# Side-by-side 512-column matmuls in the first block, moved loads, and head norms with tokens on the partitions

## The chip, the cores and the metric

The kernel runs on one core of a Trainium2 chip, in one launch. The metric is the device time in microseconds, as a median of runs. Everything is fp32. A core has TensorE (matmuls, with a queue of weight loads beside it), VectorE, ScalarE, GpSimd and SyncE, each with its own instruction stream; here SyncE issues the large weight loads and GpSimd some of the rest.

## The reference

Two blocks over one sequence of T = 256 tokens, width 2048, batch 1. Cut to what matters:

```python
def first_block(x, c, ...):
    mod = silu(c) @ ada_w + ada_b                  # 2048 -> 12288; sh1, sc1, g1, sh2, sc2, g2
    h = rmsnorm(x, norm1_g) * (1 + sc1) + sh1
    q, kc, vc, ks, vs, kw, vw, g_nsa, lx, ly, ga, gb = split(h @ w_in)
    o_a = nsa_attention(...)                       # compressed, selected and window branch
    o_b = gelu(ly) * rg_lru(causal_dwconv(lx), ...)
    y = (sigmoid(ga) * (o_a @ proj_a) + sigmoid(gb) * (o_b @ proj_b)) @ w_out
    x = x + g1 * y
    h = rmsnorm(x, norm2_g) * (1 + sc2) + sh2
    gate, val = split(h @ w_up)                    # 2048 -> 2 x 6144
    x = x + g2 * ((gelu(causal_dwconv(gate)) * val) @ w_down)
    return rmsnorm(x, final_g)

def second_block(x, ...):
    q, k, v, a_gate, u, z, g_a, g_s = split(rms_norm(x) @ w_in)
    q = rms_norm(q.reshape(b, l, 16, 64), q_norm_w)     # over the 64 of each head
    k = rms_norm(k.reshape(b, l, 4, 64), k_norm_w)
    y_a = (window_attention(q, k, v) * silu(a_gate)) @ w_attn_proj
    glu_a, glu_b = split(gelu(s5_ssm(u, ...)) @ w_glu + b_glu)
    y_s = (glu_a * sigmoid(glu_b) * silu(z)) @ w_ssm_proj
    return x + (sigmoid(g_a) * y_a + sigmoid(g_s) * y_s) @ w_out
```

## The kernel before

Activations lie transposed in SBUF: features on the 128 partitions, in 16 chunks of 256 tokens. A product of fp32 precision is made of three matmuls: with a = a_hi + a_lo (each rounded to what TensorE multiplies exactly), x·w is x_hi·w_hi + x_lo·w_hi + x_hi·w_lo (L1792).

**Units and groups.** Weights stream from HBM in units of 512 KB, 256 input rows by 512 output columns, in a ring of ten slots (`wraw`) that SyncE fills in order. For each unit ScalarE writes the rounded half `whi` (L1267, four units ahead of TensorE, six buffers), VectorE the rest `wlo` (L1272, in place of the slot), and TensorE runs 24 matmuls: 2 chunks k × 4 output chunks o × 3 terms. Units make groups (`groups()`): a group has 512 output columns (four chunks) and 8 units, those of `down` 12, those with 1024 input rows 4. The order is k, v (with the compression), NSA gates, q, lx, ly, then four times ga, gb, pa, pb, then wout 0 to 3; for each of two FFN halves gate and val 0 to 5 in turn and down 0 to 3; then the second block: q2 0, kv2, u2 0, ag2 0, q2 1, u2 1, ag2 1, z2, ga2 0 to 3, pa2, gs2, gluA, gluB, ps2, wout2. Groups write to `pair0` and `pair1` in PSUM in turn (two banks each); four more banks serve the side work. After a group its evacuation (`evac`) brings PSUM to SBUF with the group's function: sigmoid on ScalarE, or a convolution with three taps on VectorE, for example, and then the split into hi and lo.

**ada.** The vector `mod` isn't computed on TensorE: rows of ada_w of 1 MB pass through two slots of the same ring, and VectorE multiplies each with silu(c) and sums (L1248), right behind the `wlo` of the unit that the row is tied to (`g.ada[s]`: slot s of group g). 32 of the 96 go ahead of the units; the others in three sets: 16 on k1, v1, q, lx, ly; 32 on ga, gb, pa, pb; 16 on gate and val 1 to 4 of the first half.

**Side jobs.** RG-LRU, NSA attention, the compression (L490 makes `blocks`, L499 multiplies them), the tables for the recurrence (`make_turns`, on GpSimd), the head norms of the second block, its attention and the recurrence (`states`) are jobs. Each is a generator with one step per unit: in each unit's turn every engine first does its part of the unit and then one step of each job that runs. `hand` gives work from one engine to another and goes on in the next unit. So the order on each engine is fixed in the program, and a late engine holds up what stands behind on its queue.

**Head norm** (`head_norm`, for q2 0, k2 and q2 1): squares, a matmul with `halves` that sums over each head's 64 partitions and spreads the sum over them (L811), a scale, the root on ScalarE (L818), RECIPROCALs of 128x256 on VectorE (L822), and one operation that multiplies (L827).

**bz and turns.** Before the recurrence GpSimd loads `turns` and `bz` (L1082, L1085) in the first step of `states`, in ag2 0; the first matmuls of the recurrence (L1097) read `bz`.

## Time and profile before

| | us |
|---|---|
| median of 3 runs | 2693.28 (2691.06 to 2696.19) |
| profiled execution | 2692.64 |
| span of its trace | 2690.9 |
| TensorE busy | 2597.1, 97% |
| VectorE busy | 1877.7, 70% |
| ScalarE busy | 1107.6, 41% |
| GpSimd busy | 227.3, 8% |

DMA moves 568.13 MB at a mean 211 GB/s. Busy time of TensorE counts matmuls that overlap in the pipeline, so a stretch of it is read by its starts: how many matmuls begin in how many microseconds. The groups of rows below are from the page (the summary of one execution), from windows (busy time of each engine in a stretch, with the granted clock of TensorE as a share of full speed), from timelines (start, length, engine, line, operation; in square brackets the idle time of the engine before it and what ended it) and from the chain of waits that ended last.

### The profile page before, as it was taken

To read this page: it belongs to the slowest core of one execution; us is meant where nothing else is said; L and a number is where in the kernel's file an instruction comes from. 1 tells how busy PE (TensorE), PEld (TensorE's weight loads), DVE (VectorE), ACT (ScalarE), POOL (GpSimd) and SP (SyncE) were. 2 spreads that over 40 slices of the span, in tenths; PEclk is the share of its full clock that TensorE was granted. 3 is DMA by queue.
4 is the path that set the end of the run, shared out by engine and by line. 5 is a ranking of instruction groups with operands and counts; after the bars stand their busy time and mean duration, and the time that the engine had idled before them with its cause. 6 is when DMAs were issued, how large, how long until landed. Compare 5 with 4: busy or idle time off the path is not lost.

```text
span 2690.9 us, 48148 instructions
## 1 busy us (share of the span) xinstructions
PE 2597.1 (97%) x20256; PEld 2505.2 (93%) x20256; DVE 1877.7 (70%) x2519; ACT 1107.6 (41%) x1381; POOL 227.3 (8%) x190
## 2 busy tenths in 40 slices
PE   7999999989999999899999999999999999999999
PEld 5789999889999999899999999999999888899999
DVE  7865667676866674679976556654487898898563
ACT  1033456455333344444443344444444444534432
POOL 0000000000000001000466610001100000000000
PEclk9988999999999999999999999999999999999999
DMA  9974466456888886478866766665555554465664
GB/s 404 424 269 151 156 204 188 142 157 212 274 268 275 278 276 211 134 254 274 278 225 212 221 211 181 183 185 180 165 181 180 157 162 132 149 189 176 195 197 134
DMA packets 243462, 568.13 MB, mean 211 GB/s; under 512 B 17424, under 2 KB 21520, under 8 KB 228784
## 3 DMA queue, kind: packets, MB, share of 16 engines
q1 hardware_dynamic: 233776, 530.33, 60.9%
q0 software_dynamic: 9472, 34.74, 3.6%
q8 instruction: 160, 2.62, 0.4%
q14 instruction: 54, 0.44, 0.1%
...
## 4 chain that ended last, share of the span: by engine, by line
PE 75%; DVE 12%; DVEq 4%; DMA 3%; ACT 3%; issue 2%; SPq 0%; ACTq 0%; POOL 0%
PE pair L1792 65%; DVE wlo L1272 4%; DMA wraw<-ada_wT_dram 3%; ACT whi L1267 2%; DVE wraw L1248 1%; PE pair L1365 1%; PE bank L499 1%; PE pair L1798 1%; DVEq L338 1%; PE pair L1785 1%; PE states_in L684 1%; PE bank L1365 1%; PE states_in L1370 1%; PE states_in L1097 0%; PE pair L1803 0%
## 5 line engine op out<-in xcount | busy, mean ns | idle before, releaser
L1272 DVE TENSOR_TENSOR wlo<-wraw,whi 128x1024 fp32r<-128x1024 f32 x777 | 977.6, 1267 | 586.0 <-ACT whi L1267 559.5
L1267 ACT ACTIVATE whi<-wraw 128x1024 fp32r<-128x1024 f32 x777 | 813.4, 1057 | 1163.9 <-PE pair L1792 669.7
L1792 PE MATMUL pair<-h_hi,whi 128*128 128x256 f32 x3936 | 1136.3, 289 | 22.2 <-DVE h_lo L426 9.2
L1792 PE MATMUL pair<-h_lo,whi 128*128 128x256 f32 x3936 | 1121.5, 285 | 0.0
L1792 PE MATMUL pair<-h_hi,wlo 128*128 128x256 f32 x3936 | 1120.8, 285 | 0.0
L1792 PEld LDWEIGHTS pair<-h_hi,whi 128*128 128x128 f32 x3936 | 763.6, 194 | 41.5 <-issue 34.9
L1792 PEld LDWEIGHTS pair<-h_lo,whi 128*128 128x128 f32 x3936 | 763.9, 194 | 0.6
L1792 PEld LDWEIGHTS pair<-h_hi,wlo 128*128 128x128 f32 x3936 | 763.1, 194 | 0.0
L1248 DVE SCALAR_TENSOR_TENSOR wraw<-wraw,cb 128x2048 f32<-128x2048 f32 x96 | 221.4, 2309 | 58.1 <-DMA wraw<-ada_wT_dram 56.8
L1792 PE MATMUL pair<-hid_hi,whi 128*128 128x256 f32 x768 | 218.5, 284 | 0.0
L1792 PE MATMUL pair<-hid_hi,wlo 128*128 128x256 f32 x768 | 217.3, 283 | 0.0
L1792 PE MATMUL pair<-hid_lo,whi 128*128 128x256 f32 x768 | 217.3, 283 | 0.0
L1792 PEld LDWEIGHTS pair<-hid_lo,whi 128*128 128x128 f32 x768 | 147.4, 192 | 0.2
L1792 PEld LDWEIGHTS pair<-hid_hi,whi 128*128 128x128 f32 x768 | 147.4, 192 | 0.2
L1792 PEld LDWEIGHTS pair<-hid_hi,wlo 128*128 128x128 f32 x768 | 147.4, 192 | 0.0
L1792 PE MATMUL pair<-m_hi,whi 128*128 128x256 f32 x512 | 145.5, 284 | 0.0
L1792 PE MATMUL pair<-m_lo,whi 128*128 128x256 f32 x512 | 144.9, 283 | 0.0
L1792 PE MATMUL pair<-m_hi,wlo 128*128 128x256 f32 x512 | 144.9, 283 | 0.0
L1792 PEld LDWEIGHTS pair<-m_lo,whi 128*128 128x128 f32 x512 | 98.3, 192 | 0.1
L1792 PEld LDWEIGHTS pair<-m_hi,whi 128*128 128x128 f32 x512 | 98.3, 192 | 0.1
L1792 PEld LDWEIGHTS pair<-m_hi,wlo 128*128 128x128 f32 x512 | 98.3, 192 | 0.0
L1365 PEld LDWEIGHTS pair<-h_f,wfour 128*128 128x128 f32 x256 | 49.1, 195 | 29.0 <-issue 22.6
...
## 6 DMA issues: line engine op xcount, KB each, us to landing
wraw<-w_in_dram SPq DMA_DIRECT2D x312, 512.0 KB, 3.7
...
wraw<-ffn_up_dram SPq DMA_DIRECT2D x192, 512.0 KB, 3.7
...
```

Source lines behind the costliest of these rows:

```text
L338: return ve.drain() if self.me == "dve" else None
L499: ins = te.matmul(bank[1][:, 0, 0:60], wcmp[which][:, l, :], blocks[:, l, :], start=(l == 0), stop=(l == 31))
L684: te.matmul(bank[3][:, 0, :], vv(br, 0), pt[:, br, 0:T], start=False, stop=False, skip_group_check=True)
L1248: ve.scalar_tensor_tensor(out=row, in0=row, scalar=1.0, in1=cb[:, :], op0=ALU.mult, op1=ALU.mult, accum_out=mod[:, col:col + 1]).then_inc( ...
L1267: sc.activation(whi[:, r, 0:w], wraw[:, PLACE[z], 0:w], ACT.Copy).then_inc(hi_ready, 1)
L1272: ve.tensor_tensor(wlo[:, PLACE[z], 0:w], wraw[:, PLACE[z], 0:w], whi[:, r, 0:w].bitcast(F32), ALU.subtract).then_inc(lo_ready, 1)
L1365: ins = te.matmul(out, w[:, g * CB + o * P:g * CB + (o + 1) * P], x, start=(c == 0 and o % 2 == 0), stop=(c == DC - 1), skip_group_check=True)
L1370: ins = te.matmul(flat(bank[2 + b][:, :, :]), x[:, b * P:(b + 1) * P], w[:, 3 * CB:4 * CB], start=(c == 0), stop=(c == DC - 1))
L1785: ins = te.matmul(pair[:, 2 * b, 0:48], x[:, b * P:(b + 1) * P], w[:, k * 48:(k + 1) * 48], start=(k == 0 and t == 0), stop=(k == 15 and t ...
L1792: ins = te.matmul(pair[:, o, :], w[:, at_w + o * P:at_w + (o + 1) * P], x, start=(k == 0 and o % 2 == 0 and t == 0), stop=(k == last and t ...
L1798: ins = te.matmul(flat(pair[:, 2 * b:2 * b + 2, :]), x[:, b * P:(b + 1) * P], w[:, at_w:at_w + CB], start=(k == 0 and t == 0), stop=(k == ...
```

## The change

There are five parts.

1. **Wide groups.** 41 groups (pb 0 to down 3 of the first FFN half without wout, and gate and val of the second half) keep the hi and lo halves of the activations side by side, `[P, n, 2, T]`, so that one matmul of 512 columns multiplies `whi` with both, into one PSUM bank per output chunk; a matmul of 256 columns adds w_lo·x_hi to the first half of the bank. The evacuation first copies the second halves to SBUF (`tl`, ScalarE), adds the two on VectorE into `tl`, and goes on from there, two steps later than before. PSUM is cut anew for it: two areas of four banks, of which the last two serve the side work in other times.
2. **ada rows.** The first set is tied to q, ly (one each) and lx (two each), none to k1, v1. The third is tied to wout 0 (two), wout 1, wout 2 and to slot 2 of each gate and val of the first half, so also to gate 0.
3. **Head norm.** The squares are the stationary side of matmuls with two columns of `halves`, so that the sums come with tokens on the partitions, 128x16; scale, root and reciprocal work on these. VectorE spreads the result over 64 columns a head, and a matmul with the identity turns it back, from which two operations multiply q (for k2 half of each). There are two hand-offs more.
4. **First turns.** The loads of `bz` and `turns` are a job of their own, from the third unit of q2 0, ahead of the spill of outT on GpSimd's queue, `bz` first.
5. **The LRU output's last quarter** is split from `lr` itself.

TensorE in pb 0, the product of one unit; `ob` is the LRU output, `pair` and `banks` are PSUM. Before:

```order
3596 L1792 MATMUL pair<-ob_lo,whi 128x256
3597 L1792 MATMUL pair<-ob_hi,wlo 128x256
3598 L1792 MATMUL pair<-ob_hi,whi 128x256
3599 L1792 MATMUL pair<-ob_lo,whi 128x256
3600 L1792 MATMUL pair<-ob_hi,wlo 128x256
3601 L1792 MATMUL pair<-ob_hi,whi 128x256
3602 L1792 MATMUL pair<-ob_lo,whi 128x256
3603 L1792 MATMUL pair<-ob_hi,wlo 128x256
```

and of the change:

```order
2623 L1840 MATMUL banks<-ob,whi 128x512
2624 L1842 MATMUL banks<-ob,wlo 128x256
2625 L1840 MATMUL banks<-ob,whi 128x512
2626 L1842 MATMUL banks<-ob,wlo 128x256
2627 L1840 MATMUL banks<-ob,whi 128x512 [waits lo_ready]
2628 L1842 MATMUL banks<-ob,wlo 128x256
2629 L1840 MATMUL banks<-ob,whi 128x512
2630 L1842 MATMUL banks<-ob,wlo 128x256
```

Three matmuls for a product are now two.

VectorE in k1 and v1, around the first operations of the compression (`blocks`). Before:

```order
133 L1248 SCALAR_TENSOR_TENSOR wraw,mod<-wraw,cb 128x2048 [waits w_loaded8]
134 L1272 TENSOR_TENSOR wlo<-wraw,whi 128x1024 [waits hi_ready,consts_made]
135 L1416 COPY k_71<-bank 128x512 [waits pe_units]
136 L1416 COPY k_71<-bank 128x512
137 L1416 COPY v_72<-states_in 128x512 [waits pe_units]
138 L1416 COPY v_72<-states_in 128x512
139 L1272 TENSOR_TENSOR wlo<-wraw,whi 128x1024 [waits hi_ready] x2
140 L1272 TENSOR_TENSOR wlo<-wraw,whi 128x1024 [waits hi_ready,pair_freed0]
141 L1248 SCALAR_TENSOR_TENSOR wraw,mod<-wraw,cb 128x2048 [waits w_loaded4]
142 L490 TENSOR_SCALAR blocks<-kc_73,vec 128x60 x8
```

and of the change:

```order
133 L1301 TENSOR_TENSOR wlo<-wraw,whi 128x1024 [waits hi_ready,consts_made]
134 L1457 COPY k_64<-banks 128x512 [waits pe_units]
135 L1457 COPY k_64<-banks 128x512
136 L1457 COPY v_65<-banks 128x512 [waits pe_units]
137 L1457 COPY v_65<-banks 128x512
138 L1301 TENSOR_TENSOR wlo<-wraw,whi 128x1024 [waits hi_ready] x2
139 L1301 TENSOR_TENSOR wlo<-wraw,whi 128x1024 [waits hi_ready,pair_freed0]
140 L502 TENSOR_SCALAR blocks<-kc_66,vec 128x60 x8
```

The two ada operations, each of which waits for a load into the ring, are gone from ahead of `blocks`.

VectorE in the middle of the head norm of q2 0, between the recurrence's own operations (L11xx, L12xx). Before:

```order
1309 L1272 TENSOR_TENSOR wlo<-wraw,whi 128x1024 [waits hi_ready]
1310 L822 RECIPROCAL t_70<-t_70 128x256 [waits act_to_dve]
1311 L822 RECIPROCAL t_70<-t_70 128x256
1312 L1178 TENSOR_TENSOR wr<-turns_102,sy 128x512
1313 L1179 TENSOR_TENSOR wi<-turns_102,sx 128x512
1314 L1181 TENSOR_TENSOR si<-wr,wi 128x512
1315 L1272 TENSOR_TENSOR wlo<-wraw,whi 128x1024 [waits hi_ready]
1316 L822 RECIPROCAL t_70<-t_70 128x256 x2
1317 L1272 TENSOR_TENSOR wlo<-wraw,whi 128x1024 [waits hi_ready]
1318 L827 SCALAR_TENSOR_TENSOR q_104<-q_104,vec,t_70 128x1024
```

and of the change:

```order
1361 L1301 TENSOR_TENSOR wlo<-wraw,whi 128x1024 [waits hi_ready]
1362 L837 RECIPROCAL ltmp<-ltmp 128x16 [waits act_to_dve]
1363 L839 COPY t_62<-ltmp 128x1024
1364 L1207 TENSOR_TENSOR wr<-turns_95,sy 128x512
1365 L1208 TENSOR_TENSOR wi<-turns_95,sx 128x512
1366 L1210 TENSOR_TENSOR si<-wr,wi 128x512
1367 L1301 TENSOR_TENSOR wlo<-wraw,whi 128x1024 [waits hi_ready] x2
1368 L850 SCALAR_TENSOR_TENSOR q_97<-q_97,vec,banks 128x512 [waits pe_to_dve]
1369 L850 SCALAR_TENSOR_TENSOR q_97<-q_97,vec,banks 128x512
```

Four large RECIPROCALs are one small one and a copy, and the multiplication comes one unit later.

The diff, cut to its core:

```diff
-    at = [(out[of(kind, 1)], s) for kind in ("k", "v") for s in (1, 3)]
-    at += [(out[of("q", i)], 1) for i in range(4)] + [(out[of(kind, i)], 1) for i in range(4) for kind in ("lx", "ly")]
+    at = [(out[of("q", i)], 1) for i in range(4)] + [(out[of("ly", i)], 1) for i in range(4)]
+    at += [(out[of("lx", i)], s) for i in range(4) for s in (1, 3)]
...
-    at = [(out[of(kind, i)], s) for i in range(1, 5) for kind in ("gate", "val") for s in (1, 3)]
+    at = [(out[of("wout", i)], s) for i, s in ((0, 1), (0, 3), (1, 1), (2, 1))]
+    at += [(out[of(kind, i)], 2) for i in range(6) for kind in ("gate", "val")]
...
+    for g in range(of("pb", 0), of("down", 3, 0) + 1):
+        out[g].wide = out[g].kind != "wout"
+    for g in range(of("gate", 0, 1), of("val", 5, 1) + 1):
+        out[g].wide = True
...
-        return put(name + "_hi", at, [P, n, T], F32R), put(name + "_lo", at + n * 1024, [P, n, T], F32R)
+
+        both = put(name, at, [P, n, 2, T], F32R)
+        return both[:, :, 0, :], both[:, :, 1, :], both
...
-    pairs = [ctx.enter_context(nc.psum_tensor(f"pair{n}", [P, 4, T], F32)) for n in range(2)]
-    bank = [ctx.enter_context(nc.psum_tensor(f"bank{n}", [P, 2, T], F32)) for n in range(2)]
-    states_in = ctx.enter_context(nc.psum_tensor("states_in", [P, 2, 2, T], F32))
-    bank += [states_in[:, 0], states_in[:, 1]]
+
+
+    wides = [ctx.enter_context(nc.psum_tensor(f"banks{n}", [P, 4, 2, T], F32)) for n in range(2)]
+    pairs = [w[:, 0:2, :, :].rearrange("p b c t -> p (b c) t") for w in wides]
+    bank = [wides[n // 2][:, 2 + n % 2, :, :] for n in range(4)]
+    states_in = wides[1][:, 2:4, :, :]
...
+        w = 4 * n
...
-                ins = te.matmul(bank[c // 2][:, c % 2, :], halves[:, :], t1[:, c, :], start=True, stop=True)
+                for b in range(2):
+                    at = 4 * c + 2 * b
+                    ins = te.matmul(bank[0][:, 0, at:at + 2], t1[:, c, b * P:(b + 1) * P], halves[:, 0:P:64], start=True, stop=True)
         yield from j.hand("pe_to_dve", "pe", "dve", ins)
         if me == "dve":
-            for c in range(0, n, 2):
-                ins = ve.tensor_scalar(t2[:, c:c + 2, :], bank[c // 2][:, :, :], 1.0 / 64, EPS, ALU.mult, ALU.add)
+            ins = ve.tensor_scalar(hroot[:, 0:w], bank[0][:, 0, 0:w], 1.0 / 64, EPS, ALU.mult, ALU.add)
         yield from j.hand("to_act", "dve", "act", ins)
         if me == "act":
-            ins = sc.activation(t2[:, 0:n, :], t2[:, 0:n, :], ACT.Sqrt)
+            ins = sc.activation(hroot[:, 0:w], hroot[:, 0:w], ACT.Sqrt)
         yield from j.hand("act_to_dve", "act", "dve", ins)
-        for c in range(n):
-            if me == "dve":
-                ve.reciprocal(t2[:, c, :], t2[:, c, :])
-            if c % 2:
-                yield
-        if me == "dve":
-            ve.drain()
-            ve.scalar_tensor_tensor(out=src, in0=src, scalar=V(name), in1=t2[:, 0:n, :], op0=ALU.mult, op1=ALU.mult)
+        if me == "dve":
+            ve.reciprocal(hroot[:, 0:w], hroot[:, 0:w])
+            ve.drain()
+            ins = ve.tensor_copy(t1[:, 0:n, :].rearrange("p c (h r) -> p (c h) r", r=64),
+                                 hroot[:, 0:w].unsqueeze(2).broadcast_to([P, w, 64]))
+        yield from j.hand("to_pe", "dve", "pe", ins)
+        if me == "pe":
+            for c in range(n):
+                for b in range(2):
+                    ins = te.matmul(bank[c // 2][:, c % 2, b * P:(b + 1) * P], t1[:, c, b * P:(b + 1) * P], ident[:, :],
+                                    start=True, stop=True)
+        yield from j.hand("pe_to_dve", "pe", "dve", ins)
+        if me == "dve":
+            for c in range(0, n, 2):
+                ve.scalar_tensor_tensor(out=src[:, c:c + 2, :], in0=src[:, c:c + 2, :], scalar=V(name),
+                                        in1=bank[c // 2][:, :, :], op0=ALU.mult, op1=ALU.mult)
...
+    def first_turns(j):
+
         j.sync("to_pool", "dve", "pool", j.drained())
-        if me == "pool":
+        if j.me == "pool":
+            po.wait_ge(pe_units, U1[of("down", 3, 1)])
             po.wait_ge(turns_out, 256)
             for n in range(2):
+                load_bz(n)
                 load_turns(n)
-                load_bz(n)
+        yield
...
+        if gr.wide:
+
+            e, w = tl, wides[g % 2]
+            yield from j.hand("to_act", "dve", "act", j.drained())
+            if computed("act"):
+                ins = sc.activation(tl[:, :, :], w[:, :, 1, :], ACT.Copy)
+            yield from j.hand("act_to_dve", "act", "dve", ins)
+            if me == "dve":
+                done(ve.tensor_tensor(tl[:, :, :], w[:, :, 0, :], tl[:, :, :], ALU.add))
+                ve.drain()
+            done = lambda ins: ins
...
+    job(first_turns, start_of("q2", 0) + 2)
...
+                if gr.wide:
+                    for o in range(4):
+                        out, cols = wides[g % 2][:, o, :, :], slice(at_w + o * P, at_w + (o + 1) * P)
+                        te.matmul(out, wh[:, cols], X[gr.x][2][:, k, :, :], start=(k == 0), stop=(k == last),
+                                  skip_group_check=True)
+                        ins = te.matmul(out[:, 0, :], wl[:, cols], hi[:, k, :], start=False, stop=(k == last),
+                                        skip_group_check=True)
+                elif "T" in gr.mode:
```

## Rows read from the trace of the kernel before

**Rows 1.** The page, part 4: shares of the span on the chain that ended last
```profile
PE 75%; DVE 12%; DVEq 4%; DMA 3%; ACT 3%; issue 2%; SPq 0%; ACTq 0%; POOL 0%
```

**Rows 2.** Engines by stage: us, PE, PEld, DVE, ACT, POOL busy, PEclk, DMA share, GB/s
```profile
688.00:1000.00 312.00, 312.00 (x2600) 312.00 (x2601) 214.11 (x184) 122.74 (x119) 0.00 (x0) 1.00 0.82 273
1199.00:1291.00 92.00, 92.00 (x769) 92.00 (x768) 84.90 (x175) 40.10 (x43) 0.00 (x0) 1.00 0.80 274
1291.00:1318.00 27.00, 24.40 (x201) 24.05 (x201) 26.00 (x28) 8.48 (x8) 11.17 (x7) 1.00 0.75 253
1318.00:1387.00 69.00, 69.00 (x577) 69.00 (x576) 57.81 (x52) 31.51 (x35) 45.97 (x28) 1.00 0.79 261
1525.00:1802.00 277.00, 277.00 (x2311) 277.00 (x2310) 166.09 (x189) 118.80 (x127) 24.82 (x19) 1.00 0.65 193
```

**Rows 3.** Timeline of TensorE inside a 256-column unit: start us, length us
```profile
1600.24 0.28 PE L1792 MATMUL pair<-h_hi,whi 128*128 128x256 f32 x1
1600.36 0.28 PE L1792 MATMUL pair<-h_lo,whi 128*128 128x256 f32 x1
```

**Rows 4.** Timeline of TensorE, 512-column matmuls of the v group
```profile
195.14 0.39 PE L1798 MATMUL pair<-wlo,h_hi 128*128 128x512 f32 x1
...
205.11 0.39 PE L1798 MATMUL pair<-whi,h_lo 128*128 128x512 f32 x1
```

**Rows 5.** The page, part 5, and the timeline of VectorE: two prices
```profile
L1248 DVE SCALAR_TENSOR_TENSOR wraw<-wraw,cb 128x2048 f32<-128x2048 f32 x96 | 221.4, 2309 | 58.1 <-DMA wraw<-ada_wT_dram 56.8
1250.61 1.21 DVE L1500 TENSOR_TENSOR t<-t,pair 128x1024 f32<-128x1024 f32 x1
```

**Rows 6.** Timelines of VectorE and TensorE in gate 4 of the first half
```profile
1303.15 2.13 DVE L1272 TENSOR_TENSOR wlo<-wraw,whi 128x1024 fp32r<-128x1024 f32 x1 [0.18 <-issue]
1311.12 0.36 PE L1792 MATMUL pair<-h_hi,whi 128*128 128x256 f32 x1 [2.15 <-DVE wlo L1272]
```

**Rows 7.** Timelines of VectorE and TensorE in gate 0 of the first half
```profile
1113.31 1.23 DVE L1272 TENSOR_TENSOR wlo<-wraw,whi 128x1024 fp32r<-128x1024 f32 x1 [0.95 <-ACT whi L1267]
1117.28 1.23 DVE L1272 TENSOR_TENSOR wlo<-wraw,whi 128x1024 fp32r<-128x1024 f32 x1 [0.95 <-ACT whi L1267]
1116.38 0.39 PE L1792 MATMUL pair<-h_hi,whi 128*128 128x256 f32 x1 [0.62 <-DVE h_lo L426]
```

**Rows 8.** The chain in order of time, 130 to 245 us: start us, us, what
```profile
146.70 12.90 DMA wraw<-ada_wT_dram
171.24 13.91 PE bank L499 x64
185.15 6.70 PE pair L1798 x24
234.29 7.09 PE bank L499 x64
```

**Rows 9.** Timeline of TensorE, and the window of the half clock around it
```profile
171.24 1.11 PE L499 MATMUL bank<-blocks,wcmp 128*128 128x60 f32 x4 [3.57 <-DVEq L338]
170.40:187.50 17.10, 16.26 (x70) 15.78 (x71) 8.81 (x12) 2.76 (x4) 0.00 (x0) 0.50 0.03 11
```

**Rows 10.** The chain in order of time, lx 0: an ada operation on it
```profile
415.65 2.20 DVE wraw L1248
```

**Rows 11.** The start of the recurrence: timeline of TensorE, then the chain
```profile
2038.25 0.80 PE L1097 MATMUL states_in<-u,bz 32*128 32x256 f32 x2 [3.13 <-DMA bz<-B_dram]
2038.25 2.08 PE states_in L1097 x8
2040.33 25.01 PE pair L1792 x192
```

**Rows 12.** Head norms: groups by line, timeline of TensorE, then the chain
```profile
L822 DVE RECIPROCAL t<-t 128x256 f32<-128x256 f32 x10 | 16.8, 1720 | 0.1
2222.96 0.58 PE L842 MATMUL bank<-kg,q 64*128 64x128 f32 x1 [5.26 <-DVEq L338]
1989.36 1.73 PE bank L811 x8
2224.61 7.75 PE pair L1792 x48
```

48 lines of the change are left out of this document (28 added, 20 removed).

## The prediction

> **What bounds the kernel now.** I read three views of the profile in this order: the shares of the chain that ended last, the busy time by stage, and the timelines around each gap of TensorE. The chain lies on TensorE for 75% of the span and on VectorE for 12% [rows 1]. By stage, TensorE is busy without a break for 312 us and again for 277 us, in which one matmul per 0.120 us runs (2600 in 312 us) [rows 2]. There the number and width of the matmuls alone set the time, and what VectorE and ScalarE do costs nothing. So two things can bring time: cheaper matmuls, and gaps. The gaps that the change touches are few: the compression of k and v, gate 0 of the first FFN half, gate 4 of it, the start of the recurrence, and the head norm before the last attention. The prologue's 140 us and nearly all of the other gaps stay.
>
> **Wide matmuls.** The 41 wide groups have 344 units of 8 products each, 2752 in all: pb 0 to down 3 of half 0 without wout (13 + 12 + 4 groups; 104 + 96 + 48 units) and gate and val of half 1 (12 groups, 96 units). A product is now three 256-column matmuls, and becomes one of 512 columns and one of 256. The columns streamed are the same, 768; one matmul is saved. Inside a unit the 256-column matmuls start 0.12 us apart [rows 3]; 312 us for 2600 makes it 0.120 [rows 2]. The nearest row for the other form is in group v, whose matmuls take 512 columns: 44 of them lie between 195.14 and 205.11 us, so 9.97 / 44 = 0.2266 each [rows 4]. A product goes from 3 × 0.120 = 0.360 to 0.2266 + 0.120 = 0.3466, which saves 0.0133 us; × 2752 = 36.7 us. I take 13 ns, 35.8 us, and subtract the 64 products of gate 0 (0.8), where another chain sets the pace (below): **−35.0**. The two ends are −29 (if mixing the two widths costs 2 to 3 ns per product) and −37. In sentences of its own: the Trainium skill, "TensorE: Matmul & The Clock Gate", section "Back-to-back issue gap", says that back-to-back matmuls are columns / 2.4 GHz plus about 2.5 ns apart; the rows show 13 ns for both widths. By the page's figure one matmul less is worth 2.5 ns and the whole part 6.9 us, by the rows 35.8; the measurement decides.
>
> **What the wide groups add beside it.** Each of the 41 evacuations gets a ScalarE copy of the second half of the columns to SBUF and a VectorE addition before the work of before. The nearest row for a VectorE operation of 128x1024 with one operand in PSUM is 1.21 us [rows 5]; with its drain I take 1.35 us. Where TensorE is busy throughout it is hidden: in 688 to 1000 us VectorE is busy 214 of 312, in 1525 to 1802 166 of 277 [rows 2], and 1.35 + about 1.1 of waiting per group of 23 us changes neither. The banks of a group are then free two units after the next one's start, six before they are wanted. pb 3's longer end moves the issue of the x reload some 6 us, which its reader in wout 0 has as slack: 0, with 2 us if not. The split of the last quarter of the LRU output from `lr` costs a drain. The addition isn't hidden by much in the first FFN half: 84.9 of 92 us busy at 1199 to 1291 [rows 2], or 21.3 us in a group of 23.04 (192 × 0.120), and the group now takes 22.2 (64 × 0.3466). Against the addition stand the ada operations that leave. Two of these (1 MB, 2.31 us each [rows 5]) leave each gate and val group from 1 to 4 and one comes back: −2.31 + 1.35 = −1 us of VectorE per group, to which the two new hand-offs may add 1 us in which VectorE waits for ScalarE. I take 0. The one gap of that stretch, 2.15 us where matmuls wait for `wlo` [rows 6], is made by GpSimd's make_turns, next to which a VectorE subtraction takes 2.13 us where it took 1.23 [rows 6, 7]; VectorE is busy 26.0 of 27 us there, and 57.8 of 69 behind it [rows 2]. I leave it as it is: 0, with +12 (1 us in each of 12 groups not absorbed) and −3 (the gap gone) as ends.
>
> **Loads moved out of k1, v1.** In the stage of the chain from 130 to 245 us a 1 MB ada load of 12.90 us stands on the chain, and then the 64 matmuls of compress for k take 13.91 us where those for v take 7.09, and the 24 behind them 6.70 where 24 × 0.2266 = 5.44 would do [rows 8]. Before the first of them TensorE idles 3.57 us for VectorE's `blocks`, and in 170.4 to 187.5 us the granted clock is 0.50, so the level of 1.2 GHz [rows 9]. The order of VectorE shows what `blocks` waits for: an ada operation directly before them, and another some rows above, both behind late loads. With it gone, the idle time (3.57), the half clock (13.91 − 7.09 = 6.82) and its rest (1.26) should go: 11.65 in all. What stands in the way is that the weights of the next units come from the same queue, which may be the next to be late; I take **−10**, and the ends are 0 (the clock falls anyway) and −11.65. The four loads go to lx, where the chain leaves TensorE at times; one ada operation of 2.20 us stands on it in that stage [rows 10]. Four more cost between 0 and 4 × 2.31 = 9.2 us. Since one of the dozen there now is on the chain, I take that one of the four will be: **+2**.
>
> **Loads moved in the FFN.** Gate 0 of half 0 gets one. Its units are paced by a chain on VectorE of 3.97 us (1113.31 to 1117.28) with TensorE idle 0.62 us before a unit's first matmul [rows 7], so nothing hides the 2.31 us: **+2.3**. The four in wout 0 to 2 and those in the others lie beside TensorE that is busy: 0.
>
> **bz and turns earlier.** At the recurrence's start the matmuls wait 3.13 us for `bz`, and then the 8 take 2.08 us and the next 192 take 25.01 [rows 11], where 192 × 0.120 = 23.04: 3.13 + 1.04 (half of 2.08, at half clock) + 1.97 = 6.1. The loads now start at the third unit of q2 0, three groups (some 70 us) earlier. GpSimd then waits until `down` 3 of half 1 is done; what is queued behind on it is the spill of outT and later turns, whose first reader is the recurrence: 0. What is late next: the states' own VectorE chain. **−6.1**, ends 0 and −6.1.
>
> **Head norms.** A RECIPROCAL of 128x256 takes 1.72 us, and there are ten: four in each q2 norm and two in k2's [rows 12]. The one of q2 1 ends in an idle time of TensorE of 5.26 us before attention, after which 48 matmuls take 7.75 us [rows 12] instead of 5.76, so 7.3 us with the clock's part. New on VectorE: 1 of 128x16, a copy of 128x1024 and two STT of 128x512 in place of four RECIPROCALs and one STT: about 6.9 + 1.2 before, some 2.5 now, less two more hand-offs (each up to a unit's 2.9 us). The gap of 5.26 ends with VectorE's queue; 5.6 less work there is enough to close it: **−7.3**, ends 0 and −7.3. On TensorE the norm gets dearer: 8 records of the 256-column fp32 matmul take 1.73 us [rows 12]; now 8 matmuls of 2 columns and 8 of 128 columns, two records each. The nearest small-column row is 64 records of 60 columns in 7.09 us [rows 8], 111 ns each: 32 × 0.111 = 3.55, +1.8 for each of two q2 norms, +0.9 for k2: **+4.5** (0 if the small ones overlap other waits).
>
> **Sum.** −35.0 − 10 + 2 + 2.3 − 6.1 − 7.3 + 4.5 = −49.6. The profiled run took 2692.64 us (span 2690.9), 0.6 below the median of 2693.28; 2692.6 − 49.6 = 2643.0, against the median 2643.6: I predict **2644 us**.
>
> **The rivals.**
> (1) A gap closes and another takes its place. TensorE's gaps at compress, bz and the last head norm are each set by the last of several waits; what hands over instead is VectorE with its own chain. For it: in each of the three, VectorE's queue holds the waiting work [rows 8, 11, 12]. Against it: 5.6 us leave VectorE at the norm. Two of the three lost are −8 to −17 of the sum: 2652 to 2661.
> (2) VectorE sets the pace in the first FFN half. It is busy 92% there [rows 2], and faster units (22.2 instead of 23 us per group) bring it nearer. If the new hand-offs are not absorbed: +8 to +12, 2652 to 2656; with the gap at make_turns wider, up to 2664.
> (3) More is won: the gap at gate 4 goes (−3), the four loads in lx cost nothing and the norm's small matmuls fall into waits (−4): 2626 to 2636.
> (4) The matmuls' fixed cost isn't 13 ns in the mixed form, and a product keeps within 2.5 ns of its 0.360: 6.9 of 35.8 is left, 2672. For it is the page's figure alone; against it, both widths in the rows [rows 3, 4].
> (5) It doesn't do what it says: the wide matmul brings nothing and additions cost nothing; 2644 + 35 = 2679.
> (6) **Slower than before.** VectorE becomes the bound in all 25 wide groups up to down 3 of half 0 (13 + 12). This decides when a group needs over 22.2 + 4 us of VectorE: the 49.6 us saved / 12 FFN groups = 4.1 us per group. From 84.9 / 92 a group has now 21.2 us of 23, plus drains; −1 + 1 in hand-offs makes 21.2 to 23. It would need the operations slowed beside GpSimd (2.13 for 1.23 [rows 6, 7]) in the whole half, where GpSimd is busy for 57 us of the 188 [rows 2]. 2695 or more.
>
> **How the numbers follow.** The forecast (2634 to 2655) 0.55; (1) 0.15; (2) 0.13; (3) 0.08; (4) 0.04; (5) 0.02; (6) 0.02; within 0.2% (which is about what a measurement of this kernel can tell from no change, 5 us) 0.01. Range: from 2629 (most of (3)) to 2664 (all of (1) and (2)); (4) to (6) are left out. All of the cases but (6) and the last lie more than 5.4 us below 2693.28: faster 0.96, same 0.02, slower 0.02.
>
> **What would show it right or wrong.** Wide part: 8 products of a unit in 2.77 us instead of 2.88, so 104 units of pb 0 to pb 3 some 11 us shorter; wrong if the 512-column one stands 0.24 from its neighbour. Compress: 64 matmuls for k in 7.1 us at granted clock 1.00, no idle time of 3 us before; wrong if the clock is still 0.50 from 170 us. bz: the 8 state matmuls wait under 1 us. Norm: no RECIPROCAL of 128x256 left and under 1 us of idle time before the last attention. FFN: idle time of TensorE between gate 1 and val 5 of half 0 under 5 us in all; over 10 is rival (2). The forecast is wrong in its main step if TensorE's busy stretches keep 0.120 us per 256 columns.

## The result, and the profile after

| | before | after |
|---|---|---|
| median, us | 2693.65 (2691.06 to 2696.19, 5 runs) | 2667.18 (2658.68 to 2670.79, 5 runs) |
| ratio | | 0.9898, 95% interval 0.988 to 0.9915 |
| span of the profiled execution, us | 2690.9 | 2665.4 |

The change makes the kernel 1.0% faster, by 26 us, where 1.8% (49 us) was forecast, and the time lies 3 us above the range. The runs of after also lie twelve microseconds apart, those of before five.

The page of after, parts 1 and 4 (busy time, share of the span, instructions; then the chain that ended last):

```profile
PE 2570.9 (96%) x17564; PEld 2352.7 (88%) x17564; DVE 1917.3 (72%) x2556; ACT 1142.0 (43%) x1422; POOL 225.4 (8%) x190
...
PE 72%; DVE 13%; DVEq 5%; ACT 4%; issue 3%; DMA 3%; SPq 0%; ACTq 0%; POOLq 0%; POOL 0%
```

TensorE executes 2692 instructions fewer, but VectorE has more of the chain than in [rows 1]: not all of what the matmuls gave back arrives at the end.

To see where, I took from both traces the start of the first matmul of each group and subtracted. This is the length of a stretch after less its length before, in us, beside the terms of the prediction:

```
stretch                         measured   predicted
start to pa 0                       -9.6       -8.0    (compress -10, ada in lx +2)
pb 0 to pb 3          (wide)        -5.6      -11
wout 0 to 3                         +2.2        0
gate 0, half 0        (wide)        +2.1       +2.3
val 0 to val 5        (wide)        -1.2       -9
down 0 to 3, half 0   (wide)        -2.6       -5
gate, val of half 1   (wide)        -5.1      -10
down 0 to 3, half 1                  0          0
q2 0 to u2 0                        +2.8       +2.7    (small matmuls of two head norms)
ag2 0                               -5.9       -6.1    (bz)
q2 1 to ga2 0                       -4.5       -5.5    (the last head norm)
ga2 1 to the end                    +1.9        0
sum                                -25.5      -49.6
```

Six of the twelve stretches came within 1.6 us of their terms, −15.1 us together for −14.6. What failed are four of the five wide stretches, −14.5 for −35.0, with 2.2 and 1.9 us at two smaller places. The last 1.9 us needs care: 1.5 of it are in pa 2 0, a group that takes 12.8 us in some executions and 14.2 to 14.3 in others, with either head norm (below).

Windows of after in wide stretches (columns as in [rows 2]: us, then busy us and number of instructions of PE, PEld, DVE, ACT, POOL, then the granted clock, the DMA share, GB/s):

```profile
700.00:980.00 280.00, 280.00 (x1587) 242.77 (x1586) 205.70 (x177) 119.92 (x117) 0.00 (x0) 1.00 0.80 278
1120.00:1250.00 130.00, 130.00 (x751) 113.68 (x750) 105.05 (x178) 71.44 (x78) 0.00 (x0) 1.00 0.72 231
1511.00:1780.00 269.00, 269.00 (x1524) 233.39 (x1523) 179.15 (x198) 129.06 (x138) 10.55 (x10) 1.00 0.65 194
```

Two matmuls are a product. The first row gives 280 / (1587 / 2) = 0.353 us for one, the third 0.353 too, and the second 0.346. TensorE is busy all the time and the clock is granted in full in all three. From the starts of the matmuls the two values are 0.3533 and 0.3467: the second is what was forecast. So the same instructions run at one of **two paces**, 6.7 ns apart. Over the trace, by units of eight products, 262 units have the slower pace, 63 the faster, and 17 hold a stall. The pace never changes inside a stretch without a stall: slow from pb 0 (690 us), fast from val 0 (1119.5), slow, fast and slow again among the stalls of 1252 to 1355, and then slow to the end of half 1.

The stalls of the first half, on the waits of TensorE in 1252 to 1378 us (total, times, longest):

```profile
PE banks L1840 <- DVE wlo L1301: 7.3, 6, 2.2
```

and one place of VectorE's timeline in gate 4:

```profile
1286.31 1.23 DVE L1301 TENSOR_TENSOR wlo<-wraw,whi 128x1024 fp32r<-128x1024 f32 x1
1287.76 2.13 DVE L1301 TENSOR_TENSOR wlo<-wraw,whi 128x1024 fp32r<-128x1024 f32 x1 [0.23 <-issue]
1289.82 3.15 DVE L1277 SCALAR_TENSOR_TENSOR wraw<-wraw,cb 128x2048 f32<-128x2048 f32 x1
```

At 1287.75 GpSimd begins make_turns, and the same subtraction takes 2.13 instead of 1.23 us, the ada operation 3.15 instead of 2.3. Before, the waits for `wlo` in this part were 2.6 us in two, the 2.15 of [rows 6] among them; now they are 7.3 us in six. By groups, gate 4 has lost 4.0 us against its term, gate 5 2.7 and val 3 1.0.

In wout 1, VectorE's timeline and then TensorE's:

```profile
1011.93 2.29 DVE L1277 SCALAR_TENSOR_TENSOR wraw<-wraw,cb 128x2048 f32<-128x2048 f32 x1 [5.78 <-DMA wraw<-ada_wT_dram]
```

```profile
1023.51 0.70 PE L385 MATMUL banks<-t,ones 128*128 128x256 f32 x2 [1.97 <-POOLq L379]
```

VectorE stands for 5.78 us behind an ada load that the change put there, and so res, the squares on GpSimd and the sum on TensorE are late.

At the compression, the chain and two windows, and between them one window of before; then the recurrence's start and the head norm (TensorE's timelines), and the norm's operations by line:

```profile
166.50 7.09 PE banks L511 x64
```

```profile
211.40:225.10 13.70, 13.70 (x66) 13.70 (x66) 11.49 (x54) 2.59 (x3) 0.00 (x0) 0.50 0.16 51
```

```profile
195.75:216.23 20.48, 20.48 (x98) 20.48 (x98) 11.73 (x54) 2.73 (x4) 0.00 (x0) 0.50 0.10 31
170.40:187.50 17.10, 17.10 (x92) 14.67 (x92) 6.08 (x6) 5.20 (x6) 0.00 (x0) 1.00 0.29 87
```

```profile
2018.14 1.14 PE L1121 MATMUL banks<-u,bz 32*128 32x256 f32 x8
...
2170.28 1.97 PE L828 MATMUL banks<-halves,t 128*128 128x2 f32 x16 [0.79 <-DVE t L822]
```

```profile
L850 DVE SCALAR_TENSOR_TENSOR q<-q,vec,banks 128x512 f32<-128x512 f32 x4 | 2.8, 743 | 2.9 <-PE banks L845 2.9
L839 DVE COPY t<-ltmp 128x1024 f32<-128x1024 f32 (+1 forms) x3 | 1.8, 605 | 0.2
```

The 64 matmuls for k take 7.09 us (13.91 in [rows 8]) at full clock: the half clock of [rows 9] is gone. A second one, which neither [rows 9] nor the prediction shows, was there before too, in 211.40 to 225.10 us, over the second part of the NSA gates and the start of q 0. Now it begins 15.7 us earlier, 3 us after the gates do, and lasts 20.48 us for 13.70; the gates take 17.7 us for 15.0. In the other traces with the loads moved it lasts 13.7 to 20.5 us and the gates 14.9 to 17.8, so this loss varies between executions. The norm's two multiplications take 0.74 us each and the copy that spreads 0.6 on average over its two widths, where a RECIPROCAL took 1.72. The state matmuls have no wait for bz (3.13 us in [rows 11]) and take 1.14 us for 2.08.

### The profile page after: what moved, and what is told of

Read it like the earlier page. It is cut to its first block, busy times and chain, and to the rows that moved or that the text cites. A ratio compares the mean times of both kernels' runs of the same rounds, so it can differ in the third digit from the quotient of the medians.

```text
span 2665.4 us, 42959 instructions
## 1 busy us (share of the span) xinstructions
PE 2570.9 (96%) x17564; PEld 2352.7 (88%) x17564; DVE 1917.3 (72%) x2556; ACT 1142.0 (43%) x1422; POOL 225.4 (8%) x190
## 4 chain that ended last, share of the span: by engine, by line
PE 72%; DVE 13%; DVEq 5%; ACT 4%; issue 3%; DMA 3%; SPq 0%; ACTq 0%; POOLq 0%; POOL 0%
PE banks L1847 33%; PE banks L1840 20%; PE banks L1842 10%; DVE wlo L1301 5%; DMA wraw<-ada_wT_dram 2%; ACT whi L1296 2%; PE banks L1394 2%; DVEq L350 1%; PE banks L1853 1%; PE banks L1833 1%; DVE wraw L1277 1%; PE banks L511 1%; PE banks L720 1%; PE banks L696 1%; PE banks L1399 1%
## 5 line engine op out<-in xcount | busy, mean ns | idle before, releaser
L1847 PE MATMUL banks<-h,whi 128*128 128x256 f32 x4032 | 751.3, 288 | 7.8 <-DVE h L434 7.8
L1840 PE MATMUL banks<-h,whi 128*128 128x512 f32 x1920 | 679.4, 399 | 18.5 <-DVE h L438 11.2
L1847 PEld LDWEIGHTS banks<-h,whi 128*128 128x128 f32 x4032 | 635.3, 194 | 25.1 <-issue 22.7
L1847 PE MATMUL banks<-h,wlo 128*128 128x256 f32 x2016 | 573.3, 284 | 0.0
L1842 PE MATMUL banks<-h,wlo 128*128 128x256 f32 x1920 | 538.8, 281 | 0.0
L1840 PEld LDWEIGHTS banks<-h,whi 128*128 128x128 f32 x1920 | 362.0, 189 | 109.8 <-issue 16.4
L1847 PEld LDWEIGHTS banks<-h,wlo 128*128 128x128 f32 x2016 | 390.0, 193 | 0.0
L1842 PEld LDWEIGHTS banks<-h,wlo 128*128 128x128 f32 x1920 | 363.8, 189 | 0.0
L1277 DVE SCALAR_TENSOR_TENSOR wraw<-wraw,cb 128x2048 f32<-128x2048 f32 x96 | 221.9, 2314 | 35.6 <-DMA wraw<-ada_wT_dram 34.3
L1847 PE MATMUL banks<-hid,whi 128*128 128x256 f32 x768 | 139.6, 284 | 0.0
L1840 PE MATMUL banks<-hid,whi 128*128 128x512 f32 x384 | 135.7, 399 | 0.0
L1847 PEld LDWEIGHTS banks<-hid,whi 128*128 128x128 f32 x768 | 120.2, 192 | 0.4
L1847 PE MATMUL banks<-hid,wlo 128*128 128x256 f32 x384 | 108.7, 283 | 0.0
L1842 PE MATMUL banks<-hid,wlo 128*128 128x256 f32 x384 | 107.8, 281 | 0.0
L1847 PE MATMUL banks<-m,whi 128*128 128x256 f32 x512 | 92.9, 284 | 0.0
L1840 PEld LDWEIGHTS banks<-hid,whi 128*128 128x128 f32 x384 | 72.2, 188 | 18.1
```

What stands on the lines that cost most here:

```text
L1277: ve.scalar_tensor_tensor(out=row, in0=row, scalar=1.0, in1=cb[:, :], op0=ALU.mult, op1=ALU.mult, accum_out=mod[:, col:col + 1]).then_inc( ...
L1840: te.matmul(out, wh[:, cols], X[gr.x][2][:, k, :, :], start=(k == 0), stop=(k == last), skip_group_check=True)
L1842: ins = te.matmul(out[:, 0, :], wl[:, cols], hi[:, k, :], start=False, stop=(k == last), skip_group_check=True)
L1847: ins = te.matmul(pair[:, o, :], w[:, at_w + o * P:at_w + (o + 1) * P], x, start=(k == 0 and o % 2 == 0 and t == 0), stop=(k == last and t ...
```

## The experiments

Each time is set against runs of before that were taken beside it. Their median is 2692.8 for the first four experiments, 2696.2 for the next four, 2693.5 for the three behind them and 2696.5 for the last three. Where two experiments are compared, it is by these distances.

**The changed kernel once more (x1_again).** No edit.

> The changed kernel once more, for a second trace. In its first trace a product (one 512- and one 256-column matmul) takes 0.3533 us in 262 wide units and 0.3467 us in 63, and the pace changes only behind a stall of TensorE. Theory P (TensorE keeps one of two paces, taken at random when it starts again behind a stall): 2659 to 2671 us, and other stretches than before at 0.3467. Rival Q (traffic of VectorE or DMA beside it sets the pace of a stretch): the same stretches have the same pace as in the first trace (val 0 to val 3 of half 0 at 0.3467, pb 0 to pb 3 and half 1 at 0.3533), 2667 us.

Measured: 2672.86 us (2668.2 to 2674.63), 19.9 below before. The stalls of half 0 are larger: TensorE's gate 5 lasts 28.0 us (24.9 in the first trace) and down 0 36.6 (33.9). The paces lie as in the first trace, which is what Q expects and P doesn't; the time lies above both. One repetition doesn't settle it (x4_turns_late does). The waits for `wlo` are 11.3 us in seven here, for 7.3 in six, so the stall varies by some 4 us between executions.

**No wide groups (x2_narrow).**

```diff
-        out[g].wide = out[g].kind != "wout"
+        out[g].wide = False
...
-        out[g].wide = True
+        out[g].wide = False
```

> No group is wide: three 256-column matmuls a product everywhere, without the copy and addition; the rest of the change stays. From the trace of after the wide products gain 2752 x 13.3 ns = 36.6 us less 262 x 8 x 6.7 ns = 14.0 us, so 22.6. Theory A (the copies and additions made the larger stall in gate 4 and 5 of half 0, 8 us more than before): 2667 + 22.6 - 8 = 2682. Rival B (the moved loads made it): it stays, 2667 + 22.6 = 2690.

Measured: 2675.56 us, 17.2 below before. TensorE has no wait for `wlo` at all in 1252 to 1378 us, fewer than before, and 700 to 980 and 1120 to 1380 run at 0.120 us:

```profile
700.00:980.00 280.00, 280.00 (x2336) 280.00 (x2335) 188.50 (x162) 107.09 (x103) 0.00 (x0) 1.00 0.81 274
1120.00:1380.00 260.00, 260.00 (x2169) 259.96 (x2168) 211.88 (x313) 120.20 (x132) 63.68 (x39) 1.00 0.75 240
```

Theory A holds for the mechanism: GpSimd works here too, and it stalls nothing. The tables and make_turns hurt only together with the wide groups. The run takes away two things at once, though: the additions, and the faster pace of TensorE, which gives VectorE 22.2 to 22.6 us for a group where it has 23.0 here. Their shares aren't separated. In time it is 6 us below A's 2682, since I hadn't counted the 3.0 us that the gap of [rows 6] gives back when the ada loads of gate 1 to 4 are halved, and the 1.5 us of wout 1 (24.2 us here, 25.7 in after); the rest is within what executions of one kernel differ by. The wide part as shipped is thus worth only 3 to 9 us, and the rest of the change 17.

**Order of the widths (x3_hifirst).**

```diff
-                    for o in range(4):
-                        te.matmul(out, wh[:, cols], X[gr.x][2][:, k, :, :], ...)
-                        ins = te.matmul(out[:, 0, :], wl[:, cols], hi[:, k, :], ...)
+                    for o in range(4):
+                        te.matmul(wides[g % 2][:, o, :, :], wh[:, cols(o)], X[gr.x][2][:, k, :, :], ...)
+                    for o in range(4):
+                        ins = te.matmul(wides[g % 2][:, o, 0, :], wl[:, cols(o)], hi[:, k, :], ...)
```

> In a wide unit, for each k, the four 512-column matmuls come first and then the four 256-column ones, so that the widths alternate twice in eight and not eight times. Theory P (the slower pace belongs to the alternation of widths): all wide units at 4 x (0.2267 + 0.120) = 1.387 us for four products, 14 us less, 2653. Rival Q (traffic beside it): the paces of the stretches stay as in after, 2667 within 3.

Measured: 2666.23 us, 26.5 below before. The time is Q's, but the stretches show that neither holds: in all of them a product takes 0.350 or 0.351 us. The 512-column matmuls in a row start 0.229 to 0.236 us apart, not 0.2266 as in [rows 4]. The order does change the pace, to one between the two, and the stalls of half 0 stay (waits for `wlo` of 10.5 us; gate 5 27.8 us, down 0 36.2).

**make_turns later (x4_turns_late).**

```diff
-    job(make_turns, end_of("val", 3), end_of("val", 3) + 2)
-    job(output_factors, start_of("gate", 2, 1), end_of("val", 3, 1))
+    job(make_turns, start_of("down"), start_of("down") + 2)
+    job(output_factors, start_of("gate", 4, 1), end_of("val", 5, 1))
```

> GpSimd's make_turns starts with down 0 of half 0 instead of gate 4 (and the output factors on VectorE two pairs of groups later). Theory G (VectorE's operations beside GpSimd's take up to 1.7 times as long and so wlo is late in gate 4 and 5): idle time of TensorE in gate 4 to val 5 falls from about 9.8 us to under 2, 2659. Rival V (VectorE has too much work there by itself): it stays over 6 us, 2665 or more.

Measured: 2652.61 us (2648.32 to 2660.37), 40.2 below before. Its waits in 1252 to 1378, and windows of 1298 to 1378 in after and here:

```profile
PE banks L1840 <- DVE wlo L1301: 0.5, 1, 0.5
```

```profile
1298.00:1378.00 80.00, 75.54 (x422) 65.45 (x421) 74.72 (x61) 34.69 (x39) 53.37 (x33) 0.98 0.75 250
```

```profile
1298.00:1378.00 80.00, 80.00 (x463) 69.93 (x463) 63.39 (x66) 39.72 (x43) 6.95 (x5) 1.00 0.74 243
```

More matmuls run in the same 80 us, VectorE is busy 63 us for more operations instead of 75, GpSimd 7 instead of 53. Theory G holds. In the same trace the paces lie otherwise:

```profile
1125.00:1275.00 150.00, 150.00 (x851) 130.17 (x850) 122.00 (x213) 77.87 (x87) 0.00 (x0) 1.00 0.73 229
1290.00:1490.00 200.00, 200.00 (x1157) 174.90 (x1156) 147.81 (x133) 90.69 (x92) 82.76 (x58) 1.00 0.71 232
```

Here the val 0 stretch is slow (0.353) and from 1287 us, behind the one stall, all is fast (0.346) to the end of half 1, the opposite of after. The edit moves nothing ahead of gate 4, and from val 0 on the traffic is what it was (VectorE busy 81% and a DMA share of 0.72 to 0.73 in both), yet the pace is the other one. Rival Q of the first expectations, a pace set by the traffic beside it, falls by this stretch; in half 1 the traffic isn't the same (VectorE 76% for 67%, GpSimd 63 us for 11). The paces also have a part in the time: 175 units are fast here for 63 in the first trace, 112 × 8 × 6.7 ns = 6.0 of the 13.1 us between the two spans.

**The ada loads of k1 and v1 (n5_k1v1).** Edit of x2_narrow:

```diff
-    at = [(out[of("q", i)], 1) for i in range(4)] + [(out[of("ly", i)], 1) for i in range(4)]
-    at += [(out[of("lx", i)], s) for i in range(4) for s in (1, 3)]
+    at = [(out[of(kind, 1)], s) for kind in ("k", "v") for s in (1, 3)]
+    at += [(out[of("q", i)], 1) for i in range(4)] + [(out[of(kind, i)], 1) for i in range(4) for kind in ("lx", "ly")]
```

> x2_narrow (no wide groups, the rest of the change) with the first set of ada loads tied again to k1, v1, q, lx, ly. Against x2_narrow (2675.6). Theory as in the prediction (ada operations behind late loads hold up blocks, and the clock falls in the compression of k): v1 from 29.3 back to 41 us, gates 15.7 to 15.0, q to ly about 2 less, 2683 to 2685. Rival (the clock or the loads make v1 long in any case, or the loads in lx cost as much): 2676 within 3.

Measured: 2685.85 us, 10.3 below before, so 6.9 slower than x2_narrow. v1 lasts 39.7 us for 29.3. TensorE's timeline and the clock in the same stretch as above:

```profile
170.87 9.40 PE L511 MATMUL banks<-blocks,wcmp 128*128 128x60 f32 x48 [3.57 <-DVEq L350]
```

```profile
170.40:187.50 17.10, 16.63 (x77) 15.84 (x78) 8.54 (x10) 2.45 (x3) 0.00 (x0) 0.60 0.02 8
```

The idle time is the 3.57 us of [rows 9] again, and the clock falls in the compression again. That the loads hold up `blocks` and so bring the idle time and the half clock into the compression is shown.

**The head norm (n6_oldnorm).** x2_narrow with `head_norm` of before.

> x2_narrow with the head norm of the kernel before. Theory as in the prediction (the norm before the last attention costs 7.3 us at ga2 0, its new small matmuls cost 4.5 on TensorE): ga2 0 from 29.6 to 37.4 us, kv2, u2 0 and z2 1 together 5.7 less, so +2.1: 2677.7. Rival (the gap at ga2 0 belongs to the attention or the recurrence and was moved by bz and turns): ga2 0 stays at 30, and the kernel is 5 us faster, 2670.

Measured: 2681.9 us, 14.3 below before, 2.9 slower than x2_narrow. ga2 0 lasts 37.2 us for 29.6, behind this:

```profile
2209.14 0.79 PE L855 MATMUL banks<-kg,q 64*128 64x128 f32 x2 [5.25 <-DVEq L350]
```

kv2 is 1.8 shorter, u2 0 0.9, z2 1 3.4, together 6.1 where 5.7 was expected. So by the stages the new norm is worth 1.5 us: it takes away a gap of 7.6 and gives back most of it in small matmuls on TensorE, which at that point is the bound. The medians differ by 2.9, with an uncertainty of some 3 us. The two traces also differ by 1.5 us in pa 2 0 (14.3 here, 12.8 in x2_narrow). That isn't the norm's doing: the group has 12.8 us in before and 14.2 in n5_k1v1 and n7_oldturns, where a half clock of 3.4 us falls on it.

**bz and turns (n7_oldturns).** x2_narrow with the loads in `states` as before.

> x2_narrow with bz and the first turns loaded at ag2 0 as in the kernel before. Theory as in the prediction: ag2 0 from 24.3 to 30.2 us with an idle time of TensorE of 3 us that ends with bz, 2681.5. Rival (the gap goes by the shorter norm, not by the loads): ag2 0 stays under 26, 2676.

Measured: 2682.45 us, 13.7 below before, 3.5 slower than x2_narrow; ag2 0 lasts 30.2 us for 24.3, and TensorE waits for bz:

```profile
PE banks L1121 <- DMA bz<-B_dram: 3.0, 1, 3.0
```

The stage gives the forecast 5.9 us. The medians differ by 3.5 with an uncertainty of some 3 us.

**ada loads out of wout 0 (x8_wout).** Edit of x4_turns_late:

```diff
-    at = [(out[of("wout", i)], s) for i, s in ((0, 1), (0, 3), (1, 1), (2, 1))]
+    at = [(out[of("wout", i)], s) for i, s in ((1, 1), (1, 3), (2, 1), (2, 3))]
```

> x4_turns_late with the two ada loads of wout 0 tied to wout 1 and wout 2 instead. In wout 1 TensorE waits 2.7 us (in after 2.3) for the sum of squares, whose chain begins with the x reload of 2 MB and ada loads that land late. Theory D (the two ada loads beside the reload delay each other): wout 1 falls from 27.9 to 24 us, 2649. Rival I (the reload is issued later by the longer end of pb 3, and the ada loads don't matter): wout 1 stays at 26 to 28, 2652.6. The paces of TensorE may add up to 7 us either way; so the stage decides.

Measured: 2656.6 us (2648.39 to 2662.48), 39.6 below before, the same as x4_turns_late. The stage decides, as written: wout 1 lasts 23.5 us for 27.9, so without the two ada loads in wout 0 there is no gap. They can act twice, which I hadn't separated: they share the DMA with the 2 MB reload (theory D), and they hold VectorE, so that the reload itself is issued 14.5 us behind the start of wout 0 in x4_turns_late and 11.7 us here. The other traces show that the loads alone aren't enough. With the loads and no wide groups the reload is issued 8.3 to 8.5 us (n5_k1v1, n6_oldnorm) or 10.6 us behind the start (x2_narrow, n7_oldturns), and wout 1 takes 23.5 or 24.2 to 24.3; with loads and wide groups 14.4 to 14.6 us and 25.7 to 27.9. So the gap needs the loads and the late reload, theory D and rival I both, and their shares stay open. The 4.4 us went again elsewhere: in this execution val 0 to val 3 were at the fast pace, and TensorE then stalled on ssm_tables in val 3 and gate 4 (24.8 us for 22.9), to be slow from there on. The faster pace itself seems to bring VectorE nearer to being late: val 3 stalled in the three traces in which val 0 to val 2 were fast with the tables beside them, and not in the slow one.

**Everything late (x9_all_late).** Edit of the changed kernel, beside that of x8_wout:

```diff
-    at += [(out[of(kind, i)], 2) for i in range(6) for kind in ("gate", "val")]
+    at += [(out[of("val", 0)], 1), (out[of("val", 0)], 3)]
+    at += [(out[of(kind, i)], 2) for i in range(1, 6) for kind in ("gate", "val")]
...
-    job(ssm_tables, start_of("gate", 1), end_of("val", 3))
-    job(make_turns, end_of("val", 3), end_of("val", 3) + 2)
-    job(output_factors, start_of("gate", 2, 1), end_of("val", 3, 1))
+    job(ssm_tables, start_of("down"), end_of("down", 3))
+    job(make_turns, start_of("gate", 0, 1) + 1, start_of("gate", 0, 1) + 3)
+    job(output_factors, start_of("down", 1, 1), end_of("down", 2, 1))
```

> The changed kernel with every ada load and job out of the places that stalled: wout 0 has no ada load, gate 0 none (val 0 has two), ssm_tables run in down 0 to 3 of half 0, make_turns in gate and val of half 1, the output factors in down 1 and 2 of half 1. Theory P (what the wide products give is set by TensorE's pace, 0.3467 or 0.3533 us, taken at each stall; no stalls are left in half 0): wout 1 23.5, gate 0 27, gate 4 to down 0 without idle time, and 2636 (all at 0.3467) to 2654 (all at 0.3533). Rival (VectorE's additions stall TensorE also without tables and turns beside them): over 3 us of idle time between val 0 and down 0.

Measured: 2646.41 us (2645.95, 2646.06, 2646.76 and 2658.5), 47.1 below before. No wait for `wlo` stands between val 0 and down 0, wout 1 lasts 23.5 and gate 0 27.5. The profiled execution is fast from val 0 to the end of half 1:

```profile
700.00:980.00 280.00, 280.00 (x1587) 242.73 (x1586) 205.96 (x178) 120.62 (x118) 0.00 (x0) 1.00 0.81 280
1120.00:1480.00 360.00, 360.00 (x2079) 314.70 (x2078) 260.82 (x355) 172.63 (x181) 0.00 (x0) 1.00 0.69 226
```

With the wide units from val 0 on numbering 232 (88 in val 0 to val 5, 48 in down, 96 in half 1), the other pace costs 232 × 8 × 6.7 ns = 12.4 us. This is the distance of the fourth execution, 2658.5, from the other three, which fits an execution that entered val 0 at the slow pace; it has no trace, so that is inferred.

**Another bank each time (x10_lag).** Edit of x9_all_late: the 256-column matmul of chunk o − 1 comes behind the 512-column one of chunk o.

> x9_all_late with another order in the wide units: the 256-column matmul of output chunk o comes behind the 512-column one of chunk o + 1, so the widths still alternate but no two matmuls in a row write to the same bank. Theory B (the 6.7 ns of the slower pace come from two writes to one bank in a row): 0.3467 in all wide units, 2636. Rival W (they come from the widths that alternate, or from the start behind a stall): 0.350 to 0.3535 in some or all stretches, as in x9_all_late and x3_hifirst.

Measured: 2657.89 us (2653.57 to 2660.87), 35.6 below before. All wide stretches are at 0.3533. Theory B falls: with no two matmuls in a row into one bank the slow pace is there all the same.

**Narrow, without stalls (x11_narrow_late).** x9_all_late with the edit of x2_narrow.

> x9_all_late with no wide group: what the wide products are worth where nothing stalls. From x2_narrow (2675.6 beside 2692.8 of before): wout 1 and gate 0 take 3 us, 2672.6. Theory P: x9_all_late is 18 us (all wide units at 0.3533) to 36 us (all at 0.3467) faster than this one. Rival (the additions still cost on VectorE): under 15 us.

Measured: 2675.8 us (2668.45 to 2678.27), 17.7 below before. It isn't faster than x2_narrow, though gate 0 and wout 1 are 3.0 us shorter in its trace; gaps in ly 3 and pa2 0 that come and go between executions by 1.4 to 1.5 us took them back. x9_all_late is 29.4 us faster: where nothing stalls, the wide products are worth what the paces allow (18 to 36).

**Pairs (x12_pairs).** Edit of x9_all_late:

```diff
+                    for pair_ in (0, 2):
+                        for o in (pair_, pair_ + 1):
+                            te.matmul(wides[g % 2][:, o, :, :], wh[:, cols(o)], X[gr.x][2][:, k, :, :], ...)
+                        for o in (pair_, pair_ + 1):
+                            ins = te.matmul(wides[g % 2][:, o, 0, :], wl[:, cols(o)], hi[:, k, :], ...)
```

> x9_all_late with the wide matmuls in pairs: two of 512 columns, then two of 256. Theory W (each change of width may cost, so half as many changes cost half): one pace between, near 0.350 as in x3_hifirst or below, 2644 to 2650 in all executions. Rival S (the pace is a state of TensorE's pipeline and belongs to no order): again 0.3467 or 0.3533 by stretch, 2646 or 2658.

Measured: 2641.45 us (2638.21 to 2647.02), 55.0 below before, ratio to before 0.9802, interval 0.9788 to 0.9817: the fastest of all.

```profile
700.00:975.00 275.00, 275.00 (x1580) 239.94 (x1580) 204.58 (x176) 120.27 (x117) 0.00 (x0) 1.00 0.81 284
1120.00:1480.00 360.00, 360.00 (x2068) 314.13 (x2068) 260.31 (x360) 170.52 (x177) 0.00 (x0) 1.00 0.69 224
1510.00:1740.00 230.00, 230.00 (x1323) 200.71 (x1322) 192.12 (x148) 111.95 (x120) 149.88 (x102) 1.00 0.72 221
```

A product takes 0.348 us in all three rows, pb 0 to pb 3 included, which no other order brought under 0.350. A wide group of eight units lasts 22.3 us everywhere. What W expected comes true, one pace between the two in all stretches (its time, 2644 to 2650, is 3 us too high). Its reason doesn't: blocks of four have fewer changes of width still and are slower, 0.350 to 0.351. Why pairs are the best order stays open. S falls.

**Down 0 to 3 narrow (x13_down_narrow).** Edit of x9_all_late:

```diff
-        out[g].wide = out[g].kind != "wout"
+        out[g].wide = out[g].kind not in ("wout", "down")
```

> x9_all_late with down 0 to 3 of half 0 as 256-column matmuls, so that half 1's first wide group begins without a stall behind 256-column ones, as pb 0 does, which had 0.3533 in every trace. Theory E (a wide stretch that begins so has the slower pace, one that begins behind a stall may have either): gate and val of half 1 at 0.3533 whatever gate and val of half 0 have. Rival M (the pace is kept through other work until a stall): half 1 has the pace of half 0's val 0 to val 5.

Measured: 2651.76 us (two runs), 44.7 below before.

```profile
1120.00:1360.00 240.00, 240.00 (x1386) 211.73 (x1385) 176.74 (x185) 120.30 (x129) 0.00 (x0) 1.00 0.72 239
1530.00:1770.00 240.00, 240.00 (x1361) 208.26 (x1360) 200.16 (x158) 115.77 (x124) 146.87 (x99) 1.00 0.71 223
```

In the same 240 us, 1386 matmuls (0.346 us a product) in half 0 and 1361 (0.353) in half 1; the groups take 22.2 and 22.6 us. Half 1 is slow behind four narrow groups and no stall, although half 0 is fast. Theory E holds in this one trace, and M falls.

**A nudge (x14_nudge).** Edit of x9_all_late: a 16-column matmul ahead of each wide group's first.

> x9_all_late with one more matmul, of 16 columns, ahead of each wide group's first (its output is overwritten). Theory E (the pace is set by how a stretch is entered): the pace changes from group to group, with some groups of pb 0 to pb 3 at 0.3467. Rival (only a stall sets it): pb 0 to pb 3 at 0.3533 throughout and one pace from val 0 on; the matmuls cost 41 x 0.02 us, under 1 us.

Measured: 2650.7 us, 45.8 below before. pb 0 to pb 3 and val 0 to val 5 last 22.7 us a group (slow), down 0 34.0, and down 1 to 3 (33.4) and half 1 (22.3) are fast. The pace changed once in 41 groups, at the small matmul ahead of down 1, where nothing stalls. So a shift of 0.1 us can come with a change, but doesn't choose the pace, and it comes out between the two theories.

## Why the prediction was wrong

The direction and six of the twelve stretches were right. The sum was nearly twice too large, and three steps made it so; a fourth was off for a reason outside its term:

1. **"A product goes from 0.360 to 0.2266 + 0.120 = 0.3466"** was right for 63 of the 325 undisturbed wide units of the profiled execution. In the others it is 0.3533. The loss is 262 × 8 × 6.7 ns = 14.0 us, and it is the largest term. I had put 0.2266 us from a stretch of 512-column matmuls alone beside 0.120 from one of 256-column matmuls alone, and noted as an end −29 if mixing costs "2 to 3 ns per product". It costs 6.7 in the slow pace. In the same step stands the figure of 2.5 ns from the Trainium skill, "TensorE: Matmul & The Clock Gate", section "Back-to-back issue gap", which the section itself gives for an isolated matmul. Rival (4), built on it, would have left 6.9 us and is ruled out: x11_narrow_late against x9_all_late is 29.4 us. Even the slow pace leaves (0.360 − 0.3533) × 2752 = 18.4 us.
2. **"I leave it as it is: 0, with +12"** for the stall in gate 4. It grew from 2.6 us of waits for `wlo` to 7.3 in six, and with what it does to the units around it val 0 to val 5 came out 8 us above their term. This is rival (2) in its place at make_turns, at the low end of its price of 8 to 12. What I missed is the product of two things that I had both priced: the addition, and that VectorE's operations take 1.7 times as long beside GpSimd's, so that an average over the whole half (21.3 of 22.2 us) said nothing about the 120 us in which the tables and turns run. The count of −1 us of VectorE per group was also wrong for three of them: gate 5, val 5 and val 0 had no ada operation before and have one now, so that there 2.31 us are added and not taken away. x2_narrow (additions and faster pace gone) removes the waits, and x4_turns_late (make_turns gone) brings them to 0.5 us.
3. **"The four in wout 0 to 2 … lie beside TensorE that is busy: 0."** Two of them lay beside a 2 MB reload, issued 14.4 us behind the start of wout 0 where it had been 6.6 before, and VectorE waited 5.78 us: +2.2 us in the trace of after, and 4.2 to 4.4 in others. The end that I had named for this place (2 us) was for the reload alone: x8_wout took the loads away, and the gap went (23.5 us); it had needed both.
4. **Head norm, "−7.3" and "+4.5"**, −2.8 together: in its own stages it measured −2.1. ga2 0 gained 7.9 us, kv2 and u2 0 lost 1.9 and 0.9 (2.8 for a forecast of 2.7), and z2 1 lost 3.0 for 1.8, with TensorE waiting 0.79 us at L828. So the term was nearly right. The 1.9 us more behind ga2 0 are no part of it: 1.5 are the half clock in pa 2 0, which comes and goes with either norm, and no run explains the rest.

Right were: compress (v1 −11.6 us for −11.65; a longer and earlier second half clock took 2.7 back in the NSA gates, so that "−10" was near by luck, for a reason that I had not given); lx (q 0 to pa 0 came to +0.4 for +2, of parts that come and go by 1.5 us); gate 0 (+2.1 for +2.3, and gone when its ada load goes: 27.5 us in x9_all_late); bz (−5.9 for −6.1, n7_oldturns); that the 2.5 ns of the Trainium skill's section would not hold for these matmuls (13 ns in [rows 3, 4]); and the copies and additions outside the first half (0). A slip without weight: the chances of all cases but (6) and the last add up to 0.97, not 0.96.
